# Two mixture-of-experts stages of a diffusion trunk: another order of experts, another place for the output copy, unit-stride transposes

## The reference, and what it does with these inputs

```python
grp_sel = jnp.argmax(grp_logits, axis=-1)                      # one of 4 groups
top_p, top_i = lax.top_k(jax.nn.softmax(exp_logits), TOP_K)    # two of its 8 experts
y = grouped_expert_mlp(h, expert_id, w_gate, w_up, w_down)     # per expert:
#   (silu(x @ w_gate[e]) * (x @ w_up[e])) @ w_down[e]
return jnp.einsum('nk,nkd->nd', gates, y)
```

| layer | blocks of expert 0, 1, ... 31 | sum |
|---|---|---|
| 0 | 3 1 2 1 3 2 3 2 4 8 2 5 6 7 5 11 1 4 3 1 4 2 2 2 2 1 1 2 2 2 1 2 | 97 |
| 1 | 2 1 1 3 2 6 3 1 3 2 1 2 2 1 3 1 1 1 1 1 1 1 1 1 6 5 1 3 1 1 18 6 | 83 |

## Time and profile before

### The profile page before, as it was taken

The page is one execution under the profiler, slowest core; times in us unless marked ns, Lnnn a source line. Parts: engine busy times, 40 slices in busy tenths (PEclk is TensorE's granted clock), DMA queues, the critical chain, the costliest instruction groups (busy, mean ns, idle before and its releaser), DMA issues. The chain is left out here.

```text
span 5945.2 us, 98711 instructions
## 1 busy us (share of the span) xinstructions
PE 4154.5 (70%) x35526; PEld 2968.8 (50%) x35527; DVE 2348.9 (40%) x4815; ACT 1292.6 (22%) x3091; POOL 786.9 (13%) x1389
## 2 busy tenths in 40 slices
PE   5596597594958769373689873598199954576784
PEld 0385476484847658261345441487066642243342
DVE  0313544665665565433112113411777735111114
ACT  0211354342433333111000000210056611000001
POOL 0000000231313223202011112000300011111112
PEclk9798798796979889686799986699599976787897
DMA  9421100101010100343865586322500032878744
GB/s 331 142 81 70 57 9 18 27 1 33 1 24 9 24 9 0 106 141 126 336 236 199 221 332 241 130 88 78 207 26 10 10 104 92 345 298 366 302 177 141
DMA packets 237027, 765.44 MB, mean 129 GB/s; under 512 B 54560, under 2 KB 122912, under 8 KB 203984
## 3 DMA queue, kind: packets, MB, share of 16 engines
q1 hardware_dynamic: 168132, 622.14, 27.5%
q10 hardware_dynamic: 53536, 97.80, 4.5%
q0 software_dynamic: 15168, 43.03, 2.2%
HBM read 650.67 MB, written 114.83 MB: 129 GB/s over the span
## 5 line engine op out<-in xcount | busy, mean ns | idle before, releaser
L2331 PE MATMUL ex_bH<-ex_w,ex_xT 128*32 128x256 f32 x11520 | 693.6, 395 | 115.9 <-SPq L2252 80.8
L2339 PE MATMUL ex_bY<-ex_w,ex_aT 128*32 128x256 f32 x5760 | 408.8, 429 | 260.3 <-DVE ex_aT L2419 214.7
L2331 PEld LDWEIGHTS ex_bH<-ex_w,ex_xT 128*32 128x32 f32 x11520 | 376.1, 114 | 365.7 <-issue 162.3
L2339 PEld LDWEIGHTS ex_bY<-ex_w,ex_aT 128*32 128x32 f32 x5760 | 200.8, 121 | 453.9 <-issue 386.6
L2386 ACT ACTIVATE ex_sg<-ex_bH 64x256 f32<-64x256 f32 x180 | 67.5, 375 | 1567.1 <-PE ex_bH L2331 1044.4
L377 PE MATMUL p_acc<-hT,p_wh 128*128 128x512 f32 (+1 forms) x1056 | 376.3, 356 | 24.4 <-DVE p_wl L389 24.4
L377 PE MATMUL p_acc<-hT_rest,p_wh 128*128 128x512 f32 (+1 forms) x1056 | 375.9, 356 | 0.0
L377 PE MATMUL p_acc<-hT,p_wl 128*128 128x512 f32 (+1 forms) x1056 | 375.5, 356 | 0.0
L2424 DVE COPY ex_y<-ex_bY 128x256 f32<-128x256 f32 x180 | 76.3, 424 | 749.8 <-DMA yb_dram<-ex_y 553.7
L2415 DVE TENSOR_TENSOR ex_a<-ex_sg,ex_bH 64x256 f32<-64x256 f32 x180 | 76.4, 425 | 573.2 <-ACT ex_sg L2386 573.2
L713 PE MATMUL ad_S<-ad_K,ad_q 64*128 64x512 f32 (+1 forms) x768 | 191.1, 576 | 125.9 <-DMA ad_lqk<-in_od_lk 120.8
(11 more groups left out here) (352 smaller groups left out, 8172.6 us busy)
## 6 DMA issues: line engine op xcount, KB each, us to landing
ex_w<-in_moe_w_gate SPq DMA_DIRECT2D x64, 2048.0 KB, 12.0
ex_w<-in_moe_w_up SPq DMA_DIRECT2D x64, 2048.0 KB, 15.4
ex_w<-in_moe_w_down SPq DMA_DIRECT2D x64, 2048.0 KB
mods_w<-in_mod_w SPq DMA_DIRECT2D x24, 2048.0 KB
projT_dram<-p_o ACTq DMA_DIRECT2D x44, 640.0 KB, 2.9
yb_dram<-ex_y ACTq DMA_DIRECT2D x180, 128.0 KB
p_w<-in_od_w_in SPq DMA_DIRECT2D x12, 1024.0 KB, 5.1
n_x<-x_dram SPq DMA_DIRECT2D x20, 512.0 KB
```

The lines of the kernel that those rows point to most:

```text
L2331: m = nc.tensor.matmul(bH[p][g * BR:(g + 1) * BR, 0:HC], xT[:, p, e, c, :], w[:, at:at + HC], start=c == 0 and e == 0, stop=c == XG - 1 an ...
L2339: m = nc.tensor.matmul(bY[p][g * BR:(g + 1) * BR, 0:XC], aT[:, p, k % 2, k // 2, :], w[:, at:at + XC], start=k == 0, stop=k == HT - 1)
```

## The change

1. `experts_phase`, DVE: `result(b - 1, ...)` goes from second to last place in the iteration.
2. `norm_phase`, `experts_phase`: `h` is written so that the even columns of a quarter row come first and then the odd ones; the three sets of transposes then read adjacent columns. DVE's product writes `a` as two halves in the same manner, and so reads `sg` and `bH` with a step of two.
3. `route_phase`: experts are no longer taken by number. DVE ranks them by rows (32 x 32 comparisons of a key, count before number), and turns the rank r into place 2r or 63 - 2r, whichever is less: the largest expert first, the smallest second, the second largest third, and so on. Slots, table of experts and block limits follow from this place. What served to leave out experts without tokens goes.

```diff
-            placed = lambda z: z.rearrange("p (c m e) -> p m c e", c=XG, e=2)
+            placed = lambda z: z.rearrange("p (c e m) -> p m c e", c=XG, e=2)
...
-                                last = nc.tensor.transpose(tr[u][b][:, k * P:(k + 1) * P], tile, ident[:, :])
+                                last = nc.tensor.transpose(tr[u][b][:, k * P:(k + 1) * P], h[:, u, kk * P:(kk + 1) * P], ident[:, :])
...
                 tally(col(NB), rows_(count, NE, CAP), cols_(steps[:, 0:CAP], NE, CAP), ALU.is_gt, NE, CAP)
-                c.did(V.tensor_tensor_scan(col(BEND), ones[:, 0:NE], col(NB), 0.0, ALU.mult, ALU.add))
-                c.did(V.tensor_tensor(col(BST), col(BEND), col(NB), ALU.subtract))
+                c.did(V.scalar_tensor_tensor(out=col(KEY), in0=count, scalar=-float(NE), in1=iota[:, 0:NE], op0=ALU.mult, op1=ALU.add))
+                tally(col(POS), cols_(col(KEY), NE, NE), rows_(col(KEY), NE, NE), ALU.is_lt, NE, NE)
+                c.did(V.tensor_scalar(col(POS), col(POS), 2.0, None, ALU.mult))
+                c.did(V.tensor_scalar(col(ORD), col(POS), -1.0, 2.0 * NE - 1.0, ALU.mult, ALU.add))
+                c.did(V.tensor_tensor(col(ORD), col(ORD), col(POS), ALU.min))
+                tally(col(BST), cols_(col(ORD), NE, NE), rows_(col(ORD), NE, NE), ALU.is_lt, NE, NE, cols_(col(NB), NE, NE))
...
                 dve.sem_inc(slots_done, 1)
 
-                c.did(V.tensor_scalar(col(USED), col(NB), 0.0, None, ALU.is_gt))
-                c.did(V.tensor_tensor_scan(col(UC), ones[:, 0:NE], col(USED), 0.0, ALU.mult, ALU.add))
-                c.did(V.tensor_tensor(col(ORD), col(UC), col(USED), ALU.subtract))
                 tally(col(BO), cols_(col(ORD), NE, NE), rows_(iota[:, 0:NE], NE, NE), ALU.is_le, NE, NE, cols_(col(NB), NE, NE))
-                c.did(V.tensor_tensor(col(UE), col(USED), iota[:, 0:NE], ALU.mult))
...
-                c.did(V.tensor_scalar(col(USED)[:, 0:1], col(UC)[:, NE - 1:NE], 1.0, None, ALU.subtract))
...
-                        t = nc.tensor.transpose(bX[p][:, e * P:(e + 1) * P], x[:, p, e:XC:2], ident[:, :])
+                        t = nc.tensor.transpose(bX[p][:, e * P:(e + 1) * P], x[:, p, e * P:(e + 1) * P], ident[:, :])
...
-                        t = nc.tensor.transpose(bA[p][:, h * 2 * BR:(h + 1) * 2 * BR], a[2 * BR:P, p, h:HC:2], ident[2 * BR:P, 2 * BR:P])
+                        t = nc.tensor.transpose(bA[p][:, h * 2 * BR:(h + 1) * 2 * BR], a[2 * BR:P, p, h, :], ident[2 * BR:P, 2 * BR:P])
...
-                    nc.vector.tensor_tensor(a[2 * BR:P, p, :], sg[2 * BR:P, p, :], bH[p][2 * BR:P, 0:HC], ALU.mult).then_inc(a_done, 1)
+                    nc.vector.tensor_tensor(a[2 * BR:P, p, :, :], sg[2 * BR:P, p, :].rearrange("p (m h) -> p h m", h=2),
+                                            bH[p][2 * BR:P, 0:HC].rearrange("p (m h) -> p h m", h=2), ALU.mult).then_inc(a_done, 1)
...
                         product(b, p)
-                        result(b - 1, 1 - p, i)
                         hidden_turned(b, p)
                         rows_turned(b + 2, p)
+                        result(b - 1, 1 - p, i)
```

More of the change, by code:

```diff
@@ L312, in body @@
                                 kk = 4 * b + k
-                                if rows_out is None:
-                                    tile = h[:, u, kk * P:(kk + 1) * P]
-                                else:
-                                    tile = h[:, u, kk // 2 * XC + kk % 2:(kk // 2 + 1) * XC:2]
-                                last = nc.tensor.transpose(tr[u][b][:, k * P:(k + 1) * P], tile, ident[:, :])
+                                last = nc.tensor.transpose(tr[u][b][:, k * P:(k + 1) * P], h[:, u, kk * P:(kk + 1) * P], ident[:, :])
                             last.then_inc(tr_done, 1)
@@ L2134, in _ @@
                 count = tb[:, T, :]
-                NB, BEND, BST, USED, UC, ORD, BO, UE = range(8)
+                NB, BST, KEY, POS, ORD, BO = range(6)
                 col = lambda i: c32[:, i, :]
@@ L2160, in _ @@
                 dve.sem_inc(slots_done, 1)
-                c.did(V.tensor_scalar(col(USED), col(NB), 0.0, None, ALU.is_gt))
-                c.did(V.tensor_tensor_scan(col(UC), ones[:, 0:NE], col(USED), 0.0, ALU.mult, ALU.add))
-                c.did(V.tensor_tensor(col(ORD), col(UC), col(USED), ALU.subtract))
                 tally(col(BO), cols_(col(ORD), NE, NE), rows_(iota[:, 0:NE], NE, NE), ALU.is_le, NE, NE, cols_(col(NB), NE, NE))
-                c.did(V.tensor_tensor(col(UE), col(USED), iota[:, 0:NE], ALU.mult))
-                tally(tf[:, T_EXP:T_EXP + NE], cols_(col(ORD), NE, NE), rows_(iota[:, 0:NE], NE, NE), ALU.is_equal, NE, NE, cols_(col(UE), NE, NE))
+                tally(tf[:, T_EXP:T_EXP + NE], cols_(col(ORD), NE, NE), rows_(iota[:, 0:NE], NE, NE), ALU.is_equal, NE, NE, cols_(iota[:, 0:NE], NE, NE))
                 c.did(V.tensor_copy(tf[:, T_PEND:T_PEND + NE], col(BO)))
@@ L2174, in _ @@
                 tally(bo[:, 0, :], cols_(col(BO), NBT, NE), rows_(iota[:, 0:NBT], NBT, NE), ALU.is_le, NBT, NE)
-                c.did(V.tensor_scalar(col(USED)[:, 0:1], col(UC)[:, NE - 1:NE], 1.0, None, ALU.subtract))
-                c.did(V.tensor_scalar(bo[:, 0, :], bo[:, 0, :], col(USED)[:, 0:1], None, ALU.min))
+                c.did(V.tensor_scalar(bo[:, 0, :], bo[:, 0, :], float(NE - 1), None, ALU.min))
                 q = NE // WR + 1
@@ L2208, in experts_phase @@
         xT = s.sb("xT", [P, 2, 2, XG, BR])
-        sg, a = s.sb("sg", [P, 2, HC]), s.sb("a", [P, 2, HC])
+        sg, a = s.sb("sg", [P, 2, HC]), s.sb("a", [P, 2, 2, P])
         aT = s.sb("aT", [P, 2, 2, 2, BR])
```

## The result

The changed kernel takes 5960.6 us (median of 7 runs, 5951.4 to 5971.1) beside 5937.4 for the kernel before (7 runs, 5933.8 to 5939.9): a ratio of 1.0037, 95% interval [1.0026, 1.0047]. That is 0.37% slower, where 1.3% faster was forecast, and outside the range. The profiled execution is the one of 5960.6; its span is 5958.8.

A forecast was written before the change was run, and what follows sets the result against it. Stores, slowed to one block in 15.4 us beside weight fetches, were taken to bound the expert phases. Phases -86, routing +13.5 and transposes -6 gave -78.5 us: 5859 us from 5937.4, range 5790 to 5925.

The forecast's parts named there:

- PE's wait about the zero fill: Layer 0: PE's wait for weights while SP issues the zero fill, 21.3 us before, was to vanish.
- The short pairs: Expert phases: pairs of places with 4 or 3 blocks were to take 40 and 35 us.
- The chain ahead of the slots: Routing on DVE: two short instructions go, nine come, all on the path: 6.8 us longer per layer.
- the price of two fetches in a row: Expert phases: cost above 6.7 us a block per pair with five or more blocks, 8.2 us (10.4 less 2.2).
- rival B: Expert phases: fetches in pairs everywhere make it slower, gain gone at 12.6 us a pair; 5981 us, chance 0.13.
- The mean of 8.4 and 12.4: Expert phases: cost of two fetches in a row before the change, from two silu stretches: 10.4 us.
- The 2.2 us that moving the copy was to save: Expert phases: with the copy last, PE stops one down product later, saving 2.2 us per pair of fetches.
- stays covered: ACT: silu behind the later store causes no delay, as the store is issued before PE's hidden product ends.
- The first pair: Start of each expert phase: priced like other long pairs, 6.7 us a block plus 8.2.
- the transposes 6 us: PE's transposes: plain weight loads instead of strided ones save 6 us in all, bounds 0 and 40.
- the norm's add: Norm on DVE: writing 1024 elements a row in the new layout was to take no longer than 1.23 us.
- Rival A: Expert phases: the copy's new place frees PE from the stores; 5650 us, chance 0.07.

The follow-up runs named there:

- e1: The changed kernel with DVE's output copy put back into second place, new order and transposes kept: 5948.4 us, ratio 1.0020.
- e2: The kernel before with only the output copy moved to last place on DVE: 5941.7 us, ratio 1.0004.
- e7: The changed kernel with four halves of `y` instead of two and the output copy back in second place: 5771.8 us, ratio 0.9731.
- e3: The kernel before with only the unit-stride transposes, including the norm's new layout: 5937.7 us, ratio 1.0000.
- e9: The changed kernel with the copy back in second place and the ranks computed but overwritten, so experts run by number: 5962.2 us, ratio 1.0034.
- e11: The changed kernel with eight halves of `y` and the output copy back in second place: 5777.4 us, ratio 0.9721.
- e8: The changed kernel with experts by falling size instead of large and small in turn, and the copy back in second place: 5929.3 us, ratio 0.9982.

## Why the prediction was wrong, point by point

**Right.** The prediction had the stores as the bound, at the rate that the weights leave them, and the runs with four halves show it. The wait turned from `aT` (0.9 us left in each layer) into `a_done` (98.6 and 112.8; "100 us or more"). PE's wait about the zero fill is gone. The short pairs: the 4-block pairs of layer 1 took 44, 35, 39, 42 and 35 us, mean 39 (forecast 40), the 3-block ones 42, 35, 35, 35 and 34, mean 36 (35). The chain ahead of the slots: 2745.65 - 2738.48 = 7.2 us of new instructions, less the two short ones that went, 6.7 (forecast 6.8). The table was ready at 2770.0, ten us before the last scatter was issued, so its shorter tail gained nothing, as forecast.

**Wrong: the price of two fetches in a row, put at 8.2 us, measured at 13.5 and 12.7.** Silu to silu, less 6.7 n, the pairs with five or more blocks measured (n: excess):

| layer | pairs |
|---|---|
| 0 | 12: 19.8, 9: 13.6, 8: 11.4, 7: 12.0, 6: 12.8, 6: 11.7, 5: 12.0, 6: 16.6, 6: 15.0, 5: 12.8, 5: 13.2, 5: 12.9, 5: 12.0 |
| 1 | 19: 14.3, 7: 12.5, 7: 11.3, 7: 13.3, 6: 12.2 |

The means are 13.5 and 12.7, above the 12.6 that rival B named as its point of decision. B's mechanism was the right one, without the price it gave to joined fetches; its time (5981) was 20 too high. The excess is 176 us in layer 0 where 13 x 8.2 = 107 were put, and 64 in layer 1 for 41: +69 and +23, nearly the whole miss. In e1, with the copy in its old place, the means are 11.9 and 12.5. So of the 5.3 us that a pair of layer 0 is dearer than forecast, 1.5 are the price before the change (11.9 for 10.4) and 3.8 the copy's place (2.2 that it did not save, and 1.6 on top); of the 4.5 of layer 1, 2.1 and 2.4. Each of these means is from one execution, so the 1.6 may be noise; that nothing was saved isn't. In the miss are three steps:

- The mean of 8.4 and 12.4 as the price before the change. With the copy second, in e1, 13 of the 18 pairs lie between 11 and 13.3 us, three above (20.0, 16.0, 14.9) and two below (4.0, 6.5). The cheap stretch was the exception. A mean of two readings was no ground; the range should have had the dearer one inside at full weight.
- The 2.2 us that moving the copy was to save. It saved none in either order (e2; the changed kernel against e1). In the stall above PE does one down product more before it stops (1.94 us), but its restart is 4.0 us long where it was 1.5. The clock costs the same: 1.8 us on the gate and up product (5.44 for 3.66), 1.7 before on the down product (3.64 for 1.94). The sentence that ACT's silu "stays covered" failed here: the product on PE that the silu waits for is over at 3059.5, and the silu begins at 3065.39, since ACT stands at the store ahead of it, and PE's transposes wait through it. The total of ACT's waits of this kind doesn't show that (167.9 us in layer 0, 167.7 before), because the silu stood behind the store before the change too; what is new is that PE has no down product left to do meanwhile.
- The first pair, treated like the others. It has the ring's filling, three fetches in a row, beside it, and in layer 0 the zero fill: 19.8 us in layer 0, 14.3 in layer 1.

Behind the three stands one bound: weights are on their way (packets of q1) for 576 to 595 us of the phase of layer 0 and 541 to 560 of that of layer 1 in all fourteen kernels, and with two halves of `y` only three copies leave in a pair of fetches of 34 us (3040.5 to 3074.9 in the changed kernel), five in the like pair of e7. At 11 us for a block written beside fetches (34 / 3), an order mostly moves the stalls about.

**The smaller terms.** Routing cost 8.3 + 7.5 = 15.8 us for 13.5; beyond the 6.8 of the chain, the read-back of the slots is issued 6.3 us after the last scatter (2787.07 - 2779.85 - 0.96) for 4.2 before (2781.24 - 2776.05 - 0.96, with SP's issue at 2781.24). Why is open. For the transposes 6 us were taken (bounds 0 and 40). No run has them without the norm's add, and with it they come to 0 [-7, +7] (e3), so 6 is neither confirmed nor refuted; 40 is out. The rule of the Trainium skill ("SBUF — State Buffer", section "Door 1: The DMA port swizzle"), float32 free up to a step of four, doesn't fit the loads: 206 ns strided, 142 plain. The norm's add was taken as equal, a term put at nothing; by tile it isn't:

```profile
L291 DVE TENSOR_TENSOR nb_h<-nb_h,nb_mod x18: 1910/1923/1937, 2654.1 to 5003.1; 128x1024 f32<-128x1024 f32 x18
```

1.92 us for 1.23, 12.6 over 18 of them, and the two norms are 1.2 and 4.3 us longer (79.8 for 78.6, 68.8 for 64.5). The add now writes neighbours 512 bytes apart where it wrote them in adjacent pairs, with a jump behind each pair. The same section of the Trainium skill has each access that crosses to a new 16-byte line pay; the row is in line with it, and nothing else here tests it. The product that reads with a step of two stayed at 0.42, as forecast.

**The sum again.** To 5859 come 62 and 24 us for the phases (868 - 806, 779 - 755; in layer 0 the short pairs give 3 back, and the 5 put for the zero fill are in the first pair's excess), 2 for the routing, 6 for the transposes, whose gain the measured phases already hold, and 5 for the norm; 4 go, since the next phase follows the last copy of layer 0 sooner (5.2 us for 9.4). That is 5954, against 5961 measured. Put the other way, from the kernel before: some 20 us for routing, norm and transposes together (e9), 0 to -8 for the order (e1 against e9), 0 to +12 for the copy (the changed kernel against e1): +23 measured. In place of a gain of 86 the two phases together stayed as they were.

**The chances.** Rival A had the end that the four-halves kernels come near, but the wrong lever: the copy's place does not free PE of the stores, more halves do, and even they end at 5772 and not at 5650. ACT's issue then blocks (230 us in all in e7), and q10 still gets one piece in four turns (46 beside 193 of q1 from 5338 to 5345 in e11); how the 122 us divide was not worked out. The Trainium skill ("DMA: Bandwidth & Descriptors", section "Queues, rings and completion order") has engines take turns between queues by the packet; no run showed the stores get a fair share by that, in pieces of 1 KB. The chance of 0.13 for slower was too little for a forecast whose sum hung on a difference of 4.4 us a pair (12.6 - 8.2), within the spread of the two readings it rested on.

## What to carry to other kernels

An order that lets an engine rest later is worth what the buffers behind it can hold: count how many blocks can leave while a burst of fetches lasts, and give that many output buffers before changing the order (four halves of `y` alone: -1.4%; with the order: -2.7%; the order alone: nothing that can be told). No run tried to make the stores themselves faster, in larger pieces or ahead of the fetches. When a wait is turned from one instruction to another, follow the release to the engine's next useful instruction through every queue it passes, with the clock: if that chain is longer by what the engine gets done ahead of it, nothing is gained. Where the sum is n times a small difference, measure that difference in many places of the trace before multiplying. And look behind the phase that you make shorter: another engine may end it.

## What the runs showed of the hardware

- The issue of a DMA on ACT can block. With two halves of `y` the longest issue of a store took 1.2 us; with four, in e7, 34 of 180 took over 1.5 us, 230 us in all and 12.4 at most, and with eight 35, 272 us and 13.6. ACT stands still at the issue, with the silu behind it. The kernels differ in how many stores can be under way; from which number on it blocks was not measured. It is what remains of the stalls with eight halves; that it alone keeps them from being better than four isn't shown.
- A DVE add that writes 1024 float32 with neighbours 512 bytes apart takes 1.92 us, one that writes adjacent pairs 1.23.
- After a stall the half clock falls on whatever PE does next, and in the two stalls shown it costs the same on a longer piece of work as on a shorter one: 1.8 us on the gate and up product (5.44 - 3.66), 1.7 on the down product (3.64 - 1.94).
- A loop of SP that only raises a semaphore takes 0.31 us a turn, 29.7 us for 97 (3602.4 to 3632.1 in e8).
